# Two moves in the order of TensorE's work: decay units and spreads in the RWKV features, and two output tiles begun beside the last attention blocks

## The reference, cut to what matters

```python
def rwkv7_features(h, mu, w_in, w_lora1, w_lora2, w0, a_lora1, a_lora2, a0, k_k, k_a):
    xx = center_shift(h)
    xs = h[:, :, None, :] + xx[:, :, None, :] * mu
    rkvz = jnp.einsum('blcd,cde->blce', xs[:, :, :4], w_in)
    r, k, v, z = rkvz[:, :, 0], rkvz[:, :, 1], rkvz[:, :, 2], rkvz[:, :, 3]
    w_lora = jnp.einsum('nblr,nre->nble', jnp.tanh(jnp.einsum('bld,ndr->nblr', xs[:, :, 4], w_lora1)), w_lora2)
    log_w = -jax.nn.softplus(-(w0[:, None, None, :] + w_lora)) - 0.5
    decay = jnp.exp(-jnp.exp(log_w.astype(jnp.float32)))
    a = jax.nn.sigmoid(a0[:, None, None, :] + jnp.einsum('nblr,nre->nble', jnp.einsum('bld,ndr->nblr', xs[:, :, 5], a_lora1), a_lora2))
    kk = split_heads(k * k_k).astype(jnp.float32)
    kk = (kk * lax.rsqrt(jnp.sum(kk * kk, axis=-1, keepdims=True) + 1e-12)).reshape(k.shape)
    k_dir = k * (1 + (a - 1) * k_a)
    return r, decay, k_dir, v, kk, a, z
...
            # MLA layer: 16 heads, 512 queries in 4 blocks of 128, 256 + 512 keys
            o_l = mla_latent_attention(q_l, k_l, v_l, k_c, v_c, cos, sin)
            x = x + gate * ((o_l * jax.nn.silu(z_l)) @ mla_w_out[j])
```

## Time and profile before

| | |
|---|---|
| median of 3 runs | 5045.04 us (5038.1 to 5050.57) |
| profiled execution, its own time | 5050.79 us |
| its span | 5049.0 us |
| PE (TensorE matmul) busy | 4816.4 us, 95% |
| DVE, ACT, POOL busy | 29%, 21%, 6% |
| DMA | 378 MB, 75 GB/s on average |
| mean granted TensorE clock | 0.975 of full speed |

### The profile page before, as it was taken

The page is one execution under the profiler, slowest core; times in us unless marked ns, Lnnn a source line. Parts: engine busy times, 40 slices in busy tenths (PEclk is TensorE's granted clock), DMA queues, the critical chain, the costliest instruction groups (busy, mean ns, idle before and its releaser), DMA issues.

```text
span 5049.0 us, 63120 instructions
## 1 busy us (share of the span) xinstructions
PE 4816.4 (95%) x27502; PEld 2642.5 (52%) x27502; DVE 1475.1 (29%) x2777; ACT 1053.9 (21%) x2046; POOL 321.6 (6%) x302
## 2 busy tenths in 40 slices
PE   8999999999999999999998989998999999899999
PEld 4444444444444445665554568786444555544444
DVE  3621110462121010000324347775102444310100
ACT  1131000123100022110214124443112333311210
POOL 1100000110000000000014100000000010000000
PEclk9999999999999999999999999999999999899999
DMA  3151212125122211111134422223111000011211
GB/s 121 59 200 68 83 62 80 61 75 192 67 75 68 82 42 59 50 50 43 62 133 134 140 70 78 78 74 114 48 47 45 26 28 32 26 43 74 82 68 58
DMA packets 91841, 378.36 MB, mean 75 GB/s; under 512 B 7985, under 2 KB 33713, under 8 KB 62129
## 3 DMA queue, kind: packets, MB, share of 16 engines
q1 hardware_dynamic: 80608, 332.92, 18.7%
q0 software_dynamic: 9808, 37.75, 2.3%
q10 hardware_dynamic: 1152, 3.67, 0.2%
HBM read 334.46 MB, written 39.85 MB: 74 GB/s over the span
## 4 chain that ended last, share of the span: by engine, by line
PE 91%; DVE 4%; ACT 2%; issue 2%; DMA 0%; POOL 0%; POOLq 0%; SPq 0%; DVEq 0%; ACTq 0%
PE ps L521 43%; PE ps L333 23%; PE ps L542 7%; PE ps L3385 2%; PE ps L1781 2%; PE ps L339 1%; PE ps L3312 1%; PE ps L990 1%; PE ps L946 1%; PE ps L3396 1%; PE ps L2477 1%; PE ps L2428 1%; PE ps L3315 1%; PE ps L3311 1%; PE ps L3313 1%
## 5 line engine op out<-in xcount | busy, mean ns | idle before, releaser
L521 PE MATMUL ps<-A,W 128*128 128x512 f32 (+1 forms) x5408 | 2174.4, 562 | 24.5 <-DVE A L493 8.8
L521 PEld LDWEIGHTS ps<-A,W 128*128 128x128 f32 x5408 | 1028.5, 191 | 1118.9 <-issue 1076.0
L333 PE MATMUL ps<-A,W 64*64 64x64 f32 (+3 forms) x3264 | 664.5, 380 | 17.3 <-DMA W<-in_rw_in 6.1
L333 PEld LDWEIGHTS ps<-A,W 128*128 128x128 f32 (+2 forms) x3264 | 351.5, 162 | 309.7 <-issue 277.9
L333 PE MATMUL ps<-A 64*64 64x64 f32 (+3 forms) x8416 | 446.6, 238 | 63.3 <-ACT A L3538 23.2
L333 PEld LDWEIGHTS ps<-A 64*64 64x64 f32 (+2 forms) x8416 | 408.5, 148 | 166.7 <-issue 94.3
L542 PE MATMUL ps<-W,A 128*128 128x512 f32 (+1 forms) x896 | 367.6, 572 | 1.8 <-ACT A L1567 1.8
L542 PEld LDWEIGHTS ps<-W,A 128*128 128x128 f32 x896 | 173.1, 194 | 191.7 <-issue 183.6
L435 ACT ACTIVATE A<-R 128x512 f32<-128x512 f32 (+1 forms) x96 | 52.6, 574 | 782.7 <-DVE R L1577 354.6
L1697 DVE SCALAR_TENSOR_TENSOR A<-ps,V,A 128x512 f32<-128x512 f32 (+1 forms) x48 | 31.0, 661 | 486.9 <-PE ps L333 486.3
L1577 DVE SCALAR_TENSOR_TENSOR R<-ps,MOD,R 128x512 f32<-128x512 f32 (+1 forms) x48 | 31.7, 662 | 439.4 <-PE ps L521 438.1
(11 more groups left out here) (358 smaller groups left out, 4210.0 us busy)
## 6 DMA issues: line engine op xcount, KB each, us to landing
W<-in_ada SPq DMA_DIRECT2D x48, 1024.0 KB, 5.3
W<-in_w_up SPq DMA_DIRECT2D x44, 1024.0 KB, 4.8
W<-in_w_down SPq DMA_DIRECT2D x32, 704.0 KB, 4.0
W<-in_w_in SPq DMA_DIRECT2D x18, 1024.0 KB, 4.8
W<-in_sgu_v SPq DMA_DIRECT2D x16, 1024.0 KB, 4.9
W<-in_sgu_u SPq DMA_DIRECT2D x16, 1024.0 KB, 4.8
W<-in_sgu_z SPq DMA_DIRECT2D x16, 1024.0 KB, 4.9
W<-in_sgu_o SPq DMA_DIRECT2D x16, 1024.0 KB, 4.7
```

The source lines that it names most:

```text
L333: r = e.matmul(out, a, b, start=start and i == 0, stop=stop and i == len(pairs) - 1, skip_group_check=loose)
L521: t = e.matmul(ps, w[:, k, c:c + mc], x(k, seg), start=k == 0, stop=k == kt - 1)
```

## The change

It has three parts, all in TensorE's program, the first also in POOL's.

1. The table `DECAYS` says which units stand behind which product: tile 0 has units 0 and 1 behind its second product as before; tiles 1, 2 and 3 have one unit behind the first product and two behind the second; tile 4 has unit 11 behind its first. Tile 5 has none. POOL's stores follow.
2. Beside k, for tiles 1 to 6, `spread(m - 1)` stands before `rates(m)` instead of behind it.
3. 26 of the 32 matmuls of the first two `ml_out` tiles (heads 0 to 12 of 16) become pieces behind the last of `pair_pe`, in groups of one and two. The other six, for heads 13 to 15, stand behind block 63. The first two sums of squares now stand both behind tile 2.

```diff
+DECAYS = {(0, True): (0, 1), (1, False): (2,), (1, True): (3, 4), (2, False): (5,), (2, True): (6, 7), (3, False): (8,),
+          (3, True): (9, 10), (4, False): (11,)}
...
     def decay(m, lo):
-        if not (lo and m < 6):
-            return
+        units = DECAYS.get((m, bool(lo)), ())
         key = "rw_l2"
         l2 = pl.W[:, pl.slot_of[key], 0:2048]
-        if m == 0:
-            e.wait_ge(*landed(pl, key))
-            e.wait_ge(*S_.lora_act.at(4))
-            e.wait_ge(*S_.shifted.at("ones"))
-        for u in (2 * m, 2 * m + 1):
+        for u in units:
+            if u == 0:
+                e.wait_ge(*landed(pl, key))
+                e.wait_ge(*S_.lora_act.at(4))
+                e.wait_ge(*S_.shifted.at("ones"))
...
+        if 0 < m < 7:
+            spread(m - 1)
         rates(m)
-        if m:
-            spread(m - 1)
+        if m == 7:
+            spread(6)
...
     for m in range(8):
-        for u in (2 * m, 2 * m + 1) if m < 6 else ():
+        for u in DECAYS.get((m, False), ()) + DECAYS.get((m, True), ()):
             e.wait_ge(*S_.decay_act.at(u, 1))
...
-    prepared = pieces(pair_pe, pl, e)
+    def begun():
+
+        n = 0
+        for m in range(2):
+            take(pl, ("ml_out", m, SC), "67")
+        for k in range(13):
+            e.wait_ge(*S_.mla_out.at(4 * k + 3))
+            for m in range(2):
+                at, key = ("ml_out", m, SC), ("ml_out", m)
+                if k == 0:
+                    e.wait_ge(*landed(pl, key))
+                    e.wait_ge(*free(pl, at))
+                e.matmul(bank(pl, at)[:, :], slab(pl, key, 2048, 16)[:, k, :], b.so[:, k, :], start=k == 0, stop=False)
+                n += 1
+                if n % 3 < 2:
+                    yield
+
+    prepared = chain(pieces(pair_pe, pl, e), begun())
...
     def residual(m, seg):
-        if m:
-            sums_pe(pl, e, ("mod", 3), LATENT, m - 1, LATENT[0])
+        for k in (0, 1) if m == 2 else (m - 1,):
+            sums_pe(pl, e, ("mod", 3), LATENT, k, LATENT[0])
 
     e.wait_ge(*S_.mla_out.at(63))
-    features_pe(pl, e, "ml_out", [("ml_out", m) for m in range(8)], 16, P, lambda k, s: b.so[:, k, :], b.xseg,
+    for m in range(2):
+        at, key = ("ml_out", m, SC), ("ml_out", m)
+        for k in range(13, 16):
+            t = e.matmul(bank(pl, at)[:, :], slab(pl, key, 2048, 16)[:, k, :], b.so[:, k, :], start=False, stop=k == 15)
+        t.then_inc(*S_.projected.next(at, slab=key))
+    features_pe(pl, e, "ml_out", [("ml_out", m) for m in range(2, 8)], 16, P, lambda k, s: b.so[:, k, :], b.xseg, begun=2,
                 ring="0123456", beside=residual)
```

More of the change, by code:

```diff
@@ L1 @@
 from contextlib import ExitStack
+from itertools import chain
 import numpy as np
```

## The result

The changed kernel takes 4992.3 us (median of 4 runs, 4983.7 to 4996.2) against 5047.5 us before (now the median of 4 runs, 5038.1 to 5050.6; the first three gave 5045.0): a ratio of 0.988, with a 95% interval of 0.9865 to 0.9899. It is faster, by 1.2%. In a second and a third comparison the ratio was 0.988 [0.9861, 0.9898] and 0.9884 [0.987, 0.9897].

A forecast was written before the change was run, and what follows sets the result against it. The prediction took TensorE, busy 4816 of 5049 us, to bound the kernel. Gains of 8.9 + 9.6 + 45.6 = 64.1 us, taken from the median of 5045.0, gave 4981 us, range 4971 to 5001.

The forecast's parts named there:

- The main case: Whole kernel: all three parts gain as worked out, 4981 us, own range 4972 to 4992; chance 75%.
- rivals 2 and 3: 2: slab late or DVE not ready, 4990 to 4999.5, 11%. 3: chain in MLA blocks grows, 8 us each, 4988.5, 5%.
- What bounds the kernel: TensorE, busy 4816 of 5049 us; time returns only from its idle, lowered clock, or other work on its path.
- Part 1, 8.9 us: Decay units in the r projection: slab wait of 6.07 us and slow tile behind it, 2.84 us, both go.
- Part 2, 9.6 us: Spreads beside k: idle 0.7 in place of 2.04 us, 1.34 gained six times, plus 1.58 of clock.
- The clock's 1.58 us: Fifth such tile beside k took 5.30 us where equals took 3.72, a clock drop behind the gap; this goes.
- Part 3, 45.6 us: MLA blocks and `ml_out`: nine blocks at 7.16 us gain 20.6, the tail 2.4, `ml_out` 22.6 us.
- The chain of 5.82 us: MLA blocks: way from scores to product over DVE and ACT, which TensorE can't shorten; 7.16 us a block with product.
- The tail: Transposes and product of block 63: 1.77 to 0.82 and 2.93 to 1.50 us at full clock, 2.4 us less.
- The sum, 64.1 us: Whole kernel: 8.9 + 9.6 + 45.6 us, taken from the median of 5045.0 to give 4981 us.
- 1 and 4: 1: clock stays down in filled MLA blocks, 5024, 4%. 4: half clock in blocks and `ml_out`, up to 5135, 3%.
- 5 falls: Rival 5: behind the changes, scan's loads or second SGU's slabs absorb the gains; 5045 at worst, 2%.

The follow-up runs named there:

- the version with two matmuls: Only the MLA blocks changed against the kernel before, with 20 `ml_out` matmuls moved, two into each of ten blocks, 12 left behind block 63: ratio 0.9911.
- the version bank by bank: Only spreads ahead of rates against the kernel before, each rate matmul waiting for its own bank only: tile 7 of r to tile 0 of v 135.07 us, one execution.
- the one with thirty: The changed kernel with each rate matmul waiting for its own bank only and 30 `ml_out` matmuls begun in the blocks, not 26: ratio 0.9871 to before.

## Why the prediction was right, and where it was off

The forecast was 4981 us, in a range of 4971 to 5001; measured were 4992.3. The direction, the mechanism of all three parts and most terms held. That the number lies in the range is in part luck. The main case had a range of its own, up to 4992, and 4992.3 is just above it; the wider range was there for rivals 2 and 3, and neither came. (The prediction puts the lower end of that own range at 7 us below the forecast; its 4972 is 9 below.)

- **What bounds the kernel**: TensorE, and so every us of its idle or slow time counted. Shown by the parts: each gain in a stretch reached the end of the span.
- **Part 1, 8.9 us**: 9.06 us. Both terms, the wait and the slow tile, are gone; ACT and the stores cost nothing.
- **Part 2, 9.6 us**: 9.03 us. The wait was put at 0.7 us and is 0.81, so a tile gains 1.23 and not 1.34. The clock's 1.58 us were right.
- **Part 3, 45.6 us**: 44.25 us. The term that was mis-sized is the block: 7.16 us in the prediction, 7.27 measured, nine times, 1.0 us (65.4 in place of 64.4). The chain of 5.82 us was exact, as the version with two matmuls shows; the product behind it takes 1.44 us and not the 1.34 read from a block in which it followed the preparation's matmuls. The tail gave 1.8 us and not 2.4 (5.77 before, 3.94 now). Its waits of 0.69 for ACT and 0.38 for DVE are the same in both traces. What the prediction missed is that the transposes went from 1.77 to 1.27 us and not to 0.82: with the clock up there is a wait of 0.25 us for DVE within them, which the trace before doesn't show. The product went from 2.93 to 1.60 and not to 1.50. `ml_out` gave 22.8 for the 22.6 that were worked out.
- **The sum, 64.1 us**: 62.3 us in the three stretches, 58.3 in the span. The step that failed is not a term of the change but the one from stretches to the whole time: the gain was taken off one median as if the rest of the executions were equal. In the traces they differed by 6.1 us ahead of the change. In the medians the gain was 55.2 us here, and 61.0 and 59.0 in the two later comparisons. Of the 11 us by which the measured median lies above the forecast, 2.5 are the fourth run of the kernel before, 1.8 the terms, and the other 7 are scatter, for which the range had allowed 11 us above its middle.
- **The rivals**: the clock stayed up in the blocks (1 and 4 fall), the waits didn't move (2 falls), the chain didn't grow with the transposes standing later (3 falls: 5.83 us, where it was 5.82), and nothing behind absorbed the gains (5 falls).
- **The pages**: on short gaps and the clock the experiments bear out the trace, and not the rule that the Trainium skill gives on the page "TensorE: Matmul & The Clock Gate" (section "Why this matters for your kernels"). Filling the gaps with useless work brought back 21.6 us, and unfilled blocks ran at the chain's 7.27 us until the clock fell. On the price of a matmul, the page "FP8 and Floating Point Precision" of the Trainium skill (section "TensorE Precision Notes") counts four passes through the array for float32; four of the 216 ns that the Trainium skill (page "TensorE: Matmul & The Clock Gate", section "Back-to-back issue gap") gives for an isolated matmul of 512 columns make 0.86 us, an estimate from both, and the rows' 0.871 us agree. The 131 ns that the same section of the Trainium skill gives for a sustained stream would make 0.52 us, and the rows don't agree with that.

## What to carry to other kernels

Read an idle gap of TensorE together with the granted clock and the duration of the matmuls right behind it: here ten gaps, 23.2 us together, cost some 20 us more in slow matmuls. Filling them with any work returned that part (21.6 us), and having useful work in them returned another 22.6. A slab's load can begin when the last reader of its slot is done, so a small reader that stands late for no reason, like the last decay unit, is worth moving forward by the length of a load. When two executions are compared, take the difference over the stretch that was changed. D to R and R to V repeated within 0.2 us over all traces with the same order, and B to O within 0.01 us with filled blocks, where the spans of the kernel before scattered by 19. Where unfilled gaps let the clock fall, as from B to O before, the stretch itself scattered by 6.5 us, and one trace isn't enough.

## What the runs showed of the hardware

- The clock's drops depend on the moment. The unfilled stretch from B to O took 200.8, 202.8, 204.3, 204.4, 204.3, 207.3 and 204.3 us in seven traces; the one filled with 26 matmuls 160.04 or 160.05 us in four. Gaps of 2.50 us were followed by half clock in some blocks and not in others; six gaps of 2.04 us, 17.5 us apart, cost 1.6 us of slow matmuls, in each of eight traces; a gap of 2.21 us at tile 7 was followed by half clock in the version bank by bank and not in the one with thirty; nine gaps of 0.73 us cost none.
- Three traces of one and the same kernel had spans of 5049.0, 5055.3 and 5067.7 us. The differences lie ahead of the features and in the RWKV scan, where the granted clock between 3400 and 3600 us was 0.98, 0.92 and 0.87 in them. Filling gaps made not only a faster but a more repeatable stretch.
- In this program a load of ACT's table didn't wait for the semaphore of the activation behind it. Timeline of ACT, changed kernel, at the place of the first spreads:

```profile
2664.17 1.28 ACT L2000 ACT_TABLE_LOAD   x1
2665.51 2.12 ACT L2000 ACTIVATE A<-ps,V 128x256 f32<-128x256 f32 x4
```

The load began at 2664.17, while the rates' matmuls began at 2664.81. The first sigmoid followed 0.06 us behind the load, so ACT lost nothing when the rates moved back by 2.3 us.
